# Expert weights in six half pieces, and the gated attention's exponentials ahead of the row copies

## The reference

```python
for e in range(N_EXPERTS):
    g_e = jnp.sum(jnp.where(idx == e, gates, 0.0), axis=-1, keepdims=True)
    y = y + g_e * swiglu(h, w1[e], w3[e], w2[e])      # (silu(h @ w1) * (h @ w3)) @ w2
```

## Time and profile before

| what | value |
|---|---|
| median of 3 runs | 2134.02 us (2122.55 to 2137.09) |
| profiled execution, its own time | 2118.47 us |
| its span | 2116.7 us |
| PE busy | 1920.3 us (91%) |
| DVE busy | 1435.0 us (68%) |
| ACT busy | 997.6 us (47%) |
| POOL busy | 241.8 us (11%) |
| read from HBM | 546.16 MB |

### The profile page before, as it was taken

One profiled execution on the slowest core, in us unless ns is written; L12 is line 12 of the kernel. 1 busy time (PEld: TensorE's weight loads), 2 busy tenths in 40 slices (PEclk: granted clock), 3 DMA queues, 4 the chain that ended last, 5 costly groups with the idle time before them and its releaser, 6 DMA issues.

```text
span 2116.7 us, 25837 instructions
## 1 busy us (share of the span) xinstructions
PE 1920.3 (91%) x9772; PEld 1481.5 (70%) x9772; DVE 1435.0 (68%) x1376; ACT 997.6 (47%) x1047; POOL 241.8 (11%) x191
## 2 busy tenths in 40 slices
PE   5998788889998984787699999999999999999998
PEld 2774344689996862446577787777877777777776
DVE  1678353445555794443588788887878888788886
ACT  1211321233322212320267677667776677766775
POOL 0159500000000496000000000000000000000000
PEclk9996687899999986877699999999999999999999
DMA  9489472455507792561189898998989989899893
GB/s 363 148 319 322 165 295 109 131 168 180 177 14 272 271 357 81 199 230 52 40 319 359 310 358 320 335 363 301 362 314 353 355 302 363 314 352 345 313 361 141
DMA packets 238515, 552.20 MB, mean 261 GB/s; under 512 B 14792, under 2 KB 43632, under 8 KB 234096
## 3 DMA queue, kind: packets, MB, share of 16 engines
q1 hardware_dynamic: 224736, 475.96, 62.7%
q0 software_dynamic: 5920, 70.23, 8.4%
q10 hardware_dynamic: 7792, 5.08, 0.8%
HBM read 546.16 MB, written 5.08 MB: 260 GB/s over the span
## 4 chain that ended last, share of the span: by engine, by line
PE 64%; POOL 10%; DVE 10%; issue 7%; ACT 6%; SPq 1%; DMA 1%; ACTq 0%; DVEq 0%; POOLq 0%
PE bank L798 15%; PE bank L800 14%; PE bank L799 14%; POOL Z L672 4%; DVE WL L1666 3%; POOL O L670 3%; PE bank L1102 3%; PE bank L766 2%; PE bank L761 2%; ACT WH L1569 2%; PE bank L1180 2%; PE bank L1001 2%; PE bank L824 2%; POOL ring_high L683 2%; PE bank L1281 1%
## 5 line engine op out<-in xcount | busy, mean ns | idle before, releaser
L1666 DVE TENSOR_TENSOR WL<-ring_low,WH 128x2048 fp32r<-128x2048 f32 x369 | 837.5, 2290 | 248.7 <-ACT WH L1569 166.1
L1569 ACT ACTIVATE WH<-ring_low 128x2048 fp32r<-128x2048 f32 x336 | 638.1, 1922 | 209.2 <-PE bank L800 208.2
L798 PE MATMUL bank<-WH,HGH 128*128 128x512 f32 x896 | 363.7, 406 | 22.0 <-DVE WL L1666 22.0
L800 PE MATMUL bank<-WH,HGL 128*128 128x512 f32 x896 | 350.4, 391 | 0.0
L799 PE MATMUL bank<-WL,HGH 128*128 128x512 f32 x896 | 349.8, 390 | 0.0
L798 PEld LDWEIGHTS bank<-WH,HGH 128*128 128x128 f32 x896 | 168.7, 188 | 68.4 <-DVE WL L1666 32.6
L800 PEld LDWEIGHTS bank<-WH,HGL 128*128 128x128 f32 x896 | 168.5, 188 | 36.5
L799 PEld LDWEIGHTS bank<-WL,HGH 128*128 128x128 f32 x896 | 168.9, 189 | 32.4
L798 PE MATMUL bank<-WH,ATH 128*128 128x512 f32 x448 | 179.4, 400 | 0.0
L800 PE MATMUL bank<-WH,ATL 128*128 128x512 f32 x448 | 174.7, 390 | 0.0
L799 PE MATMUL bank<-WL,ATH 128*128 128x512 f32 x448 | 174.6, 390 | 0.0
(11 more groups left out here) (368 smaller groups left out, 2682.2 us busy)
## 6 DMA issues: line engine op xcount, KB each, us to landing
ring_low<-moe_w SPq DMA_DIRECT2D x336, 1024.0 KB, 6.3
ring_low<-ffn_w SPq DMA_DIRECT2D x33, 1024.0 KB, 5.3
ring_low<-w_ada SPq DMA_DIRECT2D x16, 2048.0 KB, 13.7
ring_high<-w_ada SPq DMA_DIRECT2D x8, 2048.0 KB, 16.2
ring_low<-w_in SPq DMA_DIRECT2D x7, 2048.0 KB, 26.1
ring_low<-w_out SPq DMA_DIRECT2D x4, 2048.0 KB, 10.9
ring_high<-w_in SPq DMA_DIRECT2D x3, 2048.0 KB, 11.0
C<-consts SPq DMA_DIRECT2D x1, 1170.0 KB, 18.1
```

The lines of the kernel that those rows point to most:

```text
L798: mm(out, sh, mh, start=start, stop=False)
L800: return mm(out, sl, mh, start=False, stop=stop)
L1569: A(WH[:, q % NSPLIT, :], eraw[q % NRAW], ACT.Copy).then_inc(high_ready, 1)
L1666: return tt_(out, full, high.bitcast(F32), ALU.subtract)
```

## The change

WH and WL are seen as six half pieces of 1024 columns (WH2, WL2) instead of three of 2048. ACT rounds and DVE subtracts a half at a time, PE waits for a half and gives a half back, and every count of `piece_used`, `high_ready` and `low_ready` in the experts is doubled. The loads stay as they are: SP waits for the second half of the same piece. In `down` the loop over the two rows of a piece is now outside the loop over the two column halves, so that each half piece is used up before the next. In the level loop of ACT the row work of a level now comes behind that level's exponentials and ahead of the next level's, and the copies of TMV and KV8 come behind level 0's exponentials.

```diff
--- before.py
+++ after.py
@@ -103,6 +103,8 @@
 SPOS = {p: n for n, p in enumerate(STREAM)}
 NRAW = 7
 NSPLIT = 3
+HALF = PIECE // 2
+NHALF = 2 * NPC
 assert NPC % NRAW == 0 and NPC % NSPLIT == 0
 
 
@@ -361,6 +363,7 @@
         early.close()
         WH = sb("WH", [P, NSPLIT, PIECE], F32R)
         WL = sb("WL", [P, NSPLIT, PIECE], F32R)
+        WH2, WL2 = (t[:, :, :].rearrange("p n (s f) -> p (n s) f", s=2) for t in (WH, WL))
         dense = ExitStack()
 
         def sbd(name, shape, dt=F32):
@@ -615,7 +618,7 @@
                     return
                 if q == SPOS[(2, 0, 0)] - 1:
                     q += 1
-                sp.wait_ge(low_ready, p * (NE * NPC) + e * NPC + q - NRAW + 1)
+                sp.wait_ge(low_ready, p * (NE * NHALF) + e * NHALF + 2 * (q - NRAW + 1))
 
             for q in range(NRAW):
 
@@ -1194,22 +1197,23 @@
                         def at(per, n):
                             return p * (NE * per) + e * per + n
 
-                        def piece(kind, j, half):
-
-                            q = SPOS[(kind, j, half)]
-                            pe.wait_ge(low_ready, at(NPC, q + 1))
-                            n = DM if kind == 2 else COLS
-                            return [t[:, q % NSPLIT, :].rearrange("p (c n) -> p c n", n=n) for t in (WH, WL)]
+                        def half_piece(kind, j, half, part):
+
+                            n = 2 * SPOS[(kind, j, half)] + part
+                            pe.wait_ge(low_ready, at(NHALF, n + 1))
+                            w = DM if kind == 2 else COLS
+                            return [t[:, n % (2 * NSPLIT), :].rearrange("p (c n) -> p c n", n=w) for t in (WH2, WL2)]
 
                         def up(kind, j):
 
                             for half in range(2):
-                                wh, wl = piece(kind, j, half)
                                 for i in range(4):
                                     c = 4 * half + i
+                                    if i % 2 == 0:
+                                        wh, wl = half_piece(kind, j, half, i // 2)
                                     ins = three(psum[2 * (j % 2) + kind][:, :], HGH[:, c, :], HGL[:, c, :],
-                                                wh[:, i, :], wl[:, i, :], c == 0, c == KC - 1)
-                                    if i == 3:
+                                                wh[:, i % 2, :], wl[:, i % 2, :], c == 0, c == KC - 1)
+                                    if i % 2:
                                         ins.then_inc(piece_used, 1)
                                     if j == 1 and kind == 0 and c % 2:
                                         scatter(at, c - 1)
@@ -1232,16 +1236,16 @@
 
                             pe.wait_ge(turned, at(EB, j + 1))
                             for i in parts:
-                                wh, wl = piece(2, j, i)
-                                for half in range(2):
-                                    if j == 0 and i == 0:
-                                        pe.wait_ge(y_copied, at(2, 1 + half))
-                                    for k in range(2):
+                                for k in range(2):
+                                    wh, wl = half_piece(2, j, i, k)
+                                    for half in range(2):
+                                        if j == 0 and i == 0 and k == 0:
+                                            pe.wait_ge(y_copied, at(2, 1 + half))
                                         cols = slice(half * 512, (half + 1) * 512)
-                                        ins = three(psum[4 + half][:, :], ATH[:, j % 2, 2 * i + k, :], ATL[:, j % 2, 2 * i + k, :],
-                                                    wh[:, k, cols], wl[:, k, cols], j == 0 and i == 0 and k == 0,
-                                                    j == EB - 1 and i == 1 and k == 1)
-                                ins.then_inc(piece_used, 1)
+                                        ins = three(psum[4 + half][:, :], ATH[:, j % 2, 2 * i + k, :],
+                                                    ATL[:, j % 2, 2 * i + k, :], wh[:, 0, cols], wl[:, 0, cols],
+                                                    j == 0 and i == 0 and k == 0, j == EB - 1 and i == 1 and k == 1)
+                                    ins.then_inc(piece_used, 1)
 
                         for j in range(EB):
                             if j == 0:
@@ -1443,11 +1447,13 @@
 
                 act.wait_ge(ev["gla_b"], l + 1)
                 A(GX[:, :, NP:T], GX[:, :, NP:T], ACT.Exp, scale=1.0 / 16.0).then_inc(ev["gla_decays"], 1)
-                for tt in range(2):
-                    read(A(TMV[:, tt, :], job(l, f'gtv{tt}')[:, 0:GW], ACT.Copy))
-                read(A(KV8[:, :], job(l, 'gts')[0:NS, :], ACT.Copy))
                 for n in range(LEVELS):
-                    rows(l, f'lv{n}1')
+                    if n == 1:
+                        for tt in range(2):
+                            read(A(TMV[:, tt, :], job(l, f'gtv{tt}')[:, 0:GW], ACT.Copy))
+                        read(A(KV8[:, :], job(l, 'gts')[0:NS, :], ACT.Copy))
+                    if n >= 1:
+                        rows(l, f'lv{n - 1}1')
                     act.wait_ge(ev["level_diff"], l * LEVELS + n + 1)
                     e, g = halves(EX[n % 2], n), halves(GSUM, n)
                     A(e[:, :, :, 0, :], e[:, :, :, 0, :], ACT.Exp, scale=1.0 / 16.0).then_inc(ev["level_exp"], 1)
@@ -1546,7 +1552,7 @@
 
                     def copy_sum(at):
 
-                        act.wait_ge(piece_used, at(NPC, NSPLIT))
+                        act.wait_ge(piece_used, at(NHALF, 2 * NSPLIT))
                         for half in range(2):
                             A(YS[:, half * 512:(half + 1) * 512], psum[4 + half][:, :], ACT.Copy).then_inc(y_copied, 1)
 
@@ -1565,8 +1571,10 @@
 
                         def round_piece(q):
                             act.wait_ge(raw_full[q % NRAW], at(16 * (NPC // NRAW), 16 * (q // NRAW + 1)))
-                            act.wait_ge(piece_used, at(NPC, q + 1))
-                            A(WH[:, q % NSPLIT, :], eraw[q % NRAW], ACT.Copy).then_inc(high_ready, 1)
+                            for n in (2 * q, 2 * q + 1):
+                                act.wait_ge(piece_used, at(NHALF, n + 1))
+                                A(WH2[:, n % (2 * NSPLIT), :], eraw[q % NRAW][:, n % 2 * HALF:(n % 2 + 1) * HALF],
+                                  ACT.Copy).then_inc(high_ready, 1)
 
                         def round_turned(j):
                             act.wait_ge(turn_done, at(EB, j + 1))
@@ -1589,7 +1597,7 @@
                                     if j == 1:
                                         act.wait_ge(gst_done, at(1, 1))
                                         A(GST[:, :], psum[7][:, 0:T], ACT.Copy).then_inc(gst_ready, 1)
-                                    act.wait_ge(piece_used, at(NPC, SPOS[(0, j, 1)] + 1 + NSPLIT))
+                                    act.wait_ge(piece_used, at(NHALF, 2 * (SPOS[(0, j, 1)] + 1 + NSPLIT)))
                                     act.wait_ge(ea_ready, at(EB, j + 1))
                                     A(SILU[:, :], psum[2 * (j % 2)][:, :], ACT.Silu).then_inc(esilu_ready, 1)
                         for half in range(2):
@@ -2019,7 +2027,7 @@
                     d.add(V.memset(Y[:, :, :], 0.0))
                     V.memset(small(241), 0.0).then_inc(ea_ready, 1)
                     V.memset(small(242), 0.0).then_inc(scattered, KC)
-                    V.memset(small(243), 0.0).then_inc(piece_used, NSPLIT)
+                    V.memset(small(243), 0.0).then_inc(piece_used, 2 * NSPLIT)
 
 
                     logits, top, index = (t.rearrange("p (a e) -> p a e", a=3)
@@ -2117,13 +2125,15 @@
                         for q in range(NPC):
                             if q == NPC - 1:
                                 low_turned(EB - 1)
-                            dve.wait_ge(high_ready, at(NPC, q + 1))
-                            rest(WL[:, q % NSPLIT, :], eraw[q % NRAW], WH[:, q % NSPLIT, :]).then_inc(low_ready, 1)
+                            for n in (2 * q, 2 * q + 1):
+                                dve.wait_ge(high_ready, at(NHALF, n + 1))
+                                rest(WL2[:, n % (2 * NSPLIT), :], eraw[q % NRAW][:, n % 2 * HALF:(n % 2 + 1) * HALF],
+                                     WH2[:, n % (2 * NSPLIT), :]).then_inc(low_ready, 1)
                             for j in range(EB):
                                 if q == SPOS[(0, j, 0)] + 3 and j >= 1:
                                     low_turned(j - 1)
                                 if q == SPOS[(0, j, 0)] + 5:
-                                    dve.wait_ge(piece_used, at(NPC, SPOS[(1, j, 1)] + 1 + NSPLIT))
+                                    dve.wait_ge(piece_used, at(NHALF, 2 * (SPOS[(1, j, 1)] + 1 + NSPLIT)))
                                     dve.wait_ge(esilu_ready, at(EB, j + 1))
```

## The result

| kernel | median, us (lowest to highest) | runs | ratio to before, 95% interval |
|---|---|---|---|
| before | 2133.36 (2122.55 to 2137.09) | 4 | |
| changed | 2069.64 (2068.02 to 2080.89) | 4 | 0.9744 [0.9705, 0.9783] |

The change makes the kernel 2.6% faster. The profiled execution took 2068.02 us with a span of 2065.8, 50.9 less than that of before; the forecast was 33.7 less.

What follows compares the result with a forecast made beforehand. PE was taken to bound the experts, with gains only where it starves. Gains of 21.6 (halves), 10.1 (exponentials ahead of row copies) and 2 (clock) sum to 33.7 us, from 2134.0 to 2100.3; own range 2090 to 2108, widened to 2085 to 2116.

Steps and rivals of the forecast that it cites:

- the two stretches: Experts from 1057 us, PE busy 98 of 100 us; before them two layers' level loops, where PE waits for weights.
- The room at the three places: Experts: first halves ready ahead of PE by 1.0 us at the first piece, 0.9 at piece 4, 1.2 at piece 22.
- The scatter: Experts, pieces 4 to 7: PE's scatter products, waiting for DVE's additions, are late next; 0.2 us of room, slip up to 4 us.
- A: Rival: the halves close only part of the experts' gaps, half of that gain goes; 2111 us, chance 0.12.
- D: Rival: DVE becomes the bound in the experts, 135.8 us each at 1.45 us a half; 2161 us, chance 0.04.
- C: Rival: expert weights don't come faster, 129.5 us per expert at 340 GB/s; 2109 us, chance 0.08.
- B: Rival: the level loop only changes what it waits for, row copies; only the halves gain, 2112.4 us, chance 0.10.
- E: Rival: the clock stays high in the level loops, 5 us more gained, 2095 us; forecast and this together 0.66.
- 7 x 0.99 + 8 x 0.97 + 8 x 0.61 = 19.6: Experts: us gained by closing PE's gaps before the first piece, piece 4 and piece 22 of the eight experts.
- between 0 and 8, I take 2: Level loops: us gained because denser PE work spares some products at slow clock.
- four such stretches in both layers cost about 8 us: Level loops before: slow products and fill behind idle PE cost about 8 us against full clock, both layers together.
- I set the forecast against the median: Base: the 33.7 us gain was taken from the median 2134.0, not the profiled 2118.5, giving 2100.3 rather than 2084.8.

Runs made afterwards that it cites:

- experiment 5: The changed kernel with pieces in quarters of 512 columns in place of halves: 2083.95 us, ratio 0.9776 to the kernel before.
- experiment 2: The kernel before with only ACT's new order in the level loop, pieces still whole: 2097.89 us, ratio 0.9901.
- experiment 3: The changed kernel with ACT's old order at level 1 of layer 0 alone: 2071.24 us in one run, layer 0's loop 50.9 us.
- experiment 9: The changed kernel run again, unaltered: 2069.71 us; the profiled run, 2090.2, was the slowest of six.
- experiment 1: The changed kernel with ACT's old order in the level loop, so the halves alone: 2090.48 us, ratio 0.9855 to the kernel before.
- experiment 7: The changed kernel, but PE gives back both halves of a piece only at its end: 2067.48 us in one run.
- experiment 4: The kernel before with idle PE products filling its longest waits for level weights: 2113.73 us, ratio 0.9960.
- experiment 6: The changed kernel, but PE waits for both halves of a piece before using the first: 2082.06 us in one run.
- experiment 8: The changed kernel with four (layer 0) and five (layer 1) steps of fill ahead of the pair product before level 0: 2066.98 us, ratio 0.9701.
- experiment 10: The changed kernel with six (layer 0) and eight (layer 1) idle products ahead of the pair product before level 0: 2071.22 us, ratio 0.9766.

## Why the prediction was right or wrong

**Right.** The bound, the two stretches and the mechanism of each part. A half costs what was forecast: ACT 1.06 (1.04), eight subtractions of DVE take 9.17 us, so one follows after (9.17 - 1.22) / 7 = 1.14 (1.13). By the Trainium skill, "VectorE: DVE Perf Modes", section "The TRN2 errata — SBUF-src ops pay a fixed extra latency per instruction", whose formula is for a float32 addition, 1024 columns take an estimated 1.22 us. The trace agrees, 1.22 for a single subtraction. The room at the three places came within 0.1. The scatter held with halves, and experiment 5 shows that it was rightly named as next. The price of PE's added waits, put at nothing against an upper bound of 0.02 us each that stood on no row, is right: in an expert of the changed kernel the first product of a second half starts on average 0.228 us after the one before it, as products inside a half do. At the experts' first product PE's wait for DVE fell from 6.24 to 4.32 us, 1.92 less, forecast 1.95. No wait for level weights is left, and PE's waits for ROWS stayed. Of the rivals, A and D fell in the experts (1034 us in each kernel in which PE starts on a half). C fell too: 44.04 MB in 127.4 us are 346 GB/s, over the 340 that it had as its limit. B fell in experiment 2. E was right in sign, and too small.

**Wrong, in three terms of the sum.** From 33.7 to 50.9 us in the trace:

1. *"7 x 0.99 + 8 x 0.97 + 8 x 0.61 = 19.6"* was 25.9: mis-sized by 6.3. From first product to first product, an expert gained 130.9 - 127.4 = 3.5 us, not 2.6. That holds for six of the eight. The first gained 2.5, since the products behind its start ran at half clock for 5.1 us in the changed kernel and for 3.2 in the one before, which takes back about 1.0. The last gained 2.5, since no further expert's first piece stands behind it: 6 x 3.5 + 2 x 2.5 = 26. Summing what every start of PE lies beyond one step of 0.227, over one expert, gives 7.05 us before and 3.56 after. The three gaps are 2.57 of the difference. At each of them the second product also came 0.11 late (1189.18 to 1189.52), 0.34 in all. The rest, about 0.6, are mostly steps of 0.09 to 0.11 behind the first product of a piece of w2 or w1, such as 1250.92 and 1268.59; the after trace has fewer of them. I had counted waits that the views name, not all starts. That these small steps go by the same cause was not tested by itself.
2. *"between 0 and 8, I take 2"* was about 11 in the two profiles. The loops gained 22.6 where 12.1 stood. Products slowed in the trace of before and not in that of after add up to some 8 us in layer 0 (pair products 2.51, 3.09, 2.82 and 1.23 against 1.71, 1.71, 1.71 and 0.72, and the fills beside them) and 3 in layer 1. The waits themselves gave about 11, forecast 10.1. Experiment 3 shows the coupling: a wait of 2.39 costs 1.7 more in clock. The step that failed is *"since only the longer waits among them go"*: all waits for weights went, and with them slow products that stood behind waits of 0.84 and less. That each short wait has its own share is not shown; only the 2.39 was put back by itself, and six waits of 0.32 to 0.89 in layer 1 of before have a quick pair product behind them (1.71, as at 866.65). The prediction's *"four such stretches in both layers cost about 8 us"* was also a misreading: layer 0 alone holds these 8.
3. All else came to about 0.5: the stretch from layer 1's loop to the experts gave 1.9 beyond the earlier first product, the rest gave 1.4 back. The same stretch varies between 140.8 and 144.1 over the profiles of kernels with smaller pieces, and is 143.7 in experiment 2 with whole ones, so I read nothing into it.

6.3 + 10.5 + 0.5 = 17.3, within rounding the 17.2 that the forecast lacked.

**And the base.** The remaining 13.5 of the 30.7 us come from *"I set the forecast against the median"*. The sum was made for the profiled execution (2118.5); added to 2134.0 it could only fit if the slower executions stayed as much slower. In the first set the median of before lies 14.9 us above its profiled execution and that of the changed kernel 1.6 above its own. The median of before itself moved with the set: 2133.4 (4 runs), 2121.0 (16), 2133.6 (7) and 2121.4 (11). The changed kernel stood beside it in the first and the last only, with 2069.6 and 2069.7: 63.7 and 51.7 us apart, against 50.9 in the profiles. Experiment 9 shows what the spread is made of: in one execution the clock rose later in both level loops, and that was nearly all of its 22 us. That the spread of the runs of before has the same cause is likely, but not shown: only its profiled execution has a trace.

**Open.** What decides when the clock rises. With the same instructions up to 257 us it rose in layer 0's loop near 262 in six executions (before, changed, experiments 1, 2, 3 and 7) and near 277 in four (experiments 4, 5, 6 and 9). The two groups already differ ahead of the loop, here the changed kernel and then experiment 9: PE's window from 247 us (busy, clock, DMA share, GB/s), and the pair product ahead of level 0.

```profile
247.00:253.00 6.00, 5.07 (x18) 0.50 0.99 423
...
257.29 3.09 PE L1004 MATMUL bank<-Z 64*128 64x128 f32 x16 [5.22 <-DVE Z L1860]
```

```profile
247.00:253.00 6.00, 3.32 (x24) 1.00 1.00 426
...
257.43 3.09 PE L1004 MATMUL bank<-Z 64*128 64x128 f32 x16 [7.11 <-DVE Z L1860]
```

In the four the clock had been up there (0.95 to 1.00), so PE was done sooner and then stood for 7.0 to 7.2 us, in the six for 5.2. So the late rise goes with a longer stand, but that can't be the whole cause: experiment 8 has a late rise, near 275, behind a stand of 3.4, and in layer 1 PE stood for 7.11 in both executions of the changed kernel, with the rise near 842 in one and near 882 in the other. Experiments 3 and 10 agree that standing still precedes a slow stretch; in experiment 9 PE is busy for 92% of the time from 850 to 880 us, all of it at half clock. The Trainium skill, "TensorE: Matmul & The Clock Gate", section "What's actually happening", says that activity releases the throttle. That agrees with 252 us of experiment 10 and, alone, doesn't explain 850 to 880 us of experiment 9.

## What to carry to other kernels

Where a chain of engines feeds the bound one, halving the tile nearly halves the time until that engine can start (here from 1.92 + 2.29 to 1.06 + 1.22 us); it pays until the added instructions reach the next shared place (here quarters lost 12 us, most of it at the scatter, with DVE at 89%). Price a removed wait of TensorE with the clock that it may cost behind it, as a range from nothing to the slow products in the trace, and count every late start, not only the named waits. Add a difference worked out from a trace to that trace's own time, and look at several executions before taking a median of three as the base. And empty time ahead of a loop is worth background work: four and five steps of fill moved there, with the row's copy put where ACT is idle, gave another 14 us on top of the change.

## What the runs showed of the hardware that was not expected

- The granted clock of the same program differs between executions by whole stretches: 0.50 from 840 to 880 us in one, 0.88 and then 1.00 in the other; with a late rise in layer 0 too, the spans are 22 us apart. The bulk of the runs lie together (four of six between 2069.1 and 2070.0), the others 15 to 21 us above.
- After a stand of 2.39 us (experiment 3) the first 1.7 us of products still ran quick (1.71), and only the products behind these took nearly twice their time (3.58 for 1.90).
- An instruction that follows another of its kind starts before that one's duration is over: 1.14 after, for 1.22 on DVE, and (5.83 - 1.06) / 5 = 0.95 after, for 1.06 on ACT.
